# Expert gathering and scattering dealt out between weight pieces, and decode values and states in another matmul form, in a two-layer decoder step

## The reference, cut to what matters

```python
# per layer; x is prompt or sample
x = x + mixers(rmsnorm(x))        # 6 mLSTM + 6 SSD (pairs of 12 heads) + 4 retention units
x = x + cross_attn(rmsnorm(x))
x = x + ffn(rmsnorm(x))           # layer 0: dense SwiGLU; layer 1: top 2 of 8 experts
# a decode step of a mixer unit, for each of the 8 samples (all three kinds have this form)
S = decay * S + outer(v, k)       # a 128 x 128 state per sample and unit
y = S @ q
# experts
for e in range(8):
    act = silu(h @ w_gate[e]) * (h @ w_up[e])
    out = out + combine[..., e:e+1] * (act @ w_down[e])
```

## Time and profile before

| | us |
|---|---|
| median of 3 runs | 1915.89 (1913.73 to 1925.07) |
| the profiled execution | 1909.86, its span 1908.0 |
| PE busy over the span | 1808.2 (95%) |
| DVE, ACT, POOL busy | 1290.4, 1060.4, 367.7 |
| mixers' units, layer 0 and layer 1 | about 203 to 316 and 905 to 1019 |
| experts with their gatherings and scatterings | about 1236 to 1900 |

### The profile page before, as it was taken

One profiled execution on the slowest core, in us unless ns is written; L12 is line 12 of the kernel. 1 busy time (PEld: TensorE's weight loads), 2 busy tenths in 40 slices (PEclk: granted clock), 3 DMA queues, 4 the chain that ended last, 5 costly groups with the idle time before them and its releaser, 6 DMA issues.

```text
span 1908.0 us, 30795 instructions
## 1 busy us (share of the span) xinstructions
PE 1808.2 (95%) x12287; PEld 1648.4 (86%) x12287; DVE 1290.4 (68%) x1836; ACT 1060.4 (56%) x1709; POOL 367.7 (19%) x334
## 2 busy tenths in 40 slices
PE   7999989999899998999999999799899999989997
PEld 6999979997799998999989987688788888878886
DVE  4764776542556567655855533698879978978986
ACT  4445445443545454445445534377667866766775
POOL 4970332000000007932231000040012003000000
PEclk9999989999899998999979999899999999999999
DMA  7554345547655453553446367379959978986994
GB/s 296 177 172 163 122 141 182 200 170 288 226 175 193 168 207 126 191 180 134 144 124 248 134 248 292 121 267 355 358 212 350 370 259 298 363 330 228 355 363 167
DMA packets 73603, 434.07 MB, mean 227 GB/s; under 512 B 8373, under 2 KB 13045, under 8 KB 33013
## 3 DMA queue, kind: packets, MB, share of 16 engines
q1 hardware_dynamic: 71332, 425.19, 61.8%
q0 software_dynamic: 2128, 6.92, 1.0%
HBM read 407.59 MB, written 24.48 MB: 226 GB/s over the span
## 4 chain that ended last, share of the span: by engine, by line
PE 81%; DVE 10%; DMA 5%; ACT 2%; issue 1%; SPq 0%; DVEq 0%; ACTq 0%
PE ps L1134 16%; PE ps L576 14%; PE ps L577 14%; PE ps L578 13%; PE ps L1160 8%; DVE wL L301 3%; DMA ring<-x_down_dram 2%; PE ps L1117 2%; PE ps L556 2%; DVE stream L1886 2%; PE ps L816 1%; DMA ring<-x_gu_dram 1%; PE ps L1172 1%; DVE proj L1943 1%; PE ps L797 1%; ACT wH L295 1%
## 5 line engine op out<-in xcount | busy, mean ns | idle before, releaser
L301 DVE TENSOR_TENSOR wL<-ring,wH 128x1024 fp32r<-128x1024 f32 (+1 forms) x704 | 834.4, 1216 | 383.6 <-ACT wH L295 379.2
L295 ACT ACTIVATE wH<-ring 128x1024 fp32r<-128x1024 f32 (+1 forms) x704 | 709.1, 1026 | 280.2 <-PE ps L578 117.6
L576 PE MATMUL ps<-hH,wH 128*128 128x264 f32 x1376 | 400.7, 291 | 14.3 <-DVE hL L1669 7.8
L577 PE MATMUL ps<-hL,wH 128*128 128x264 f32 x1376 | 392.5, 285 | 0.0
L578 PE MATMUL ps<-hH,wL 128*128 128x264 f32 x1376 | 392.0, 285 | 0.0
L1134 PE MATMUL ps<-wH,projR 128*128 128x512 f32 (+1 forms) x1152 | 294.0, 377 | 0.3 <-ACT wH L295 0.3
L576 PEld LDWEIGHTS ps<-hH,wH 128*128 128x128 f32 x1376 | 261.1, 190 | 23.0 <-issue 19.0
L577 PEld LDWEIGHTS ps<-hL,wH 128*128 128x128 f32 x1376 | 261.7, 190 | 0.6
L578 PEld LDWEIGHTS ps<-hH,wL 128*128 128x128 f32 x1376 | 260.5, 189 | 0.0
L576 PE MATMUL ps<-projR,wH 128*128 128x264 f32 (+1 forms) x816 | 239.0, 293 | 15.8 <-DVE projR L2041 7.1
L1134 PEld LDWEIGHTS ps<-wH,projR 128*128 128x128 f32 x1152 | 211.0, 188 | 35.9 <-issue 1.4
(11 more groups left out here) (365 smaller groups left out, 2394.6 us busy)
## 6 DMA issues: line engine op xcount, KB each, us to landing
ring<-x_gu_dram SPq DMA_DIRECT2D x96, 1024.0 KB, 7.1
ring<-x_down_dram SPq DMA_DIRECT2D x60, 1024.0 KB, 7.0
ring<-w_in_dram SPq DMA_DIRECT2D x56, 1024.0 KB, 4.9
ring<-x_gu_dram SPq DMA_DIRECT2D x48, 768.0 KB, 5.7
ring<-w_gu_dram SPq DMA_DIRECT2D x22, 1024.0 KB, 4.9
stream<-states_dram SPq DMA_DIRECT2D x32, 512.0 KB, 4.2
ring<-w_out_dram SPq DMA_DIRECT2D x16, 1024.0 KB, 4.9
o_states_dram<-stream SPq DMA_DIRECT2D x32, 512.0 KB, 4.4
```

The source lines that it names most:

```text
L295: act.activation(wH[:, buf * PIECE:buf * PIECE + n], slot(s, half * n, n), ACT.Copy).then_inc(hi_ready, 1)
L301: dve.tensor_tensor(wL[:, buf * PIECE:buf * PIECE + n], slot(s, half * n, n), f32(wH[:, buf * PIECE:buf * PIECE + n]), ALU.subtract).then_ ...
L576: pe.matmul(dst, wh, high(k0 + k), start=k0 + k == 0, stop=False)
L577: pe.matmul(dst, wh, low(k0 + k), start=False, stop=False)
```

## The change

Two things are changed in one step.

**Experts.** `gather` and `scatter` take one k (of 8) at a time. PE's list puts gather k of the next group behind down piece k of the group's third item, `slot_sums` behind down piece 8, and scatter k of the last group behind gate and up piece k of the second chunk of the next group's first item. A gathering alternates between bank 7 and one gate bank instead of four banks. The last group's scattering becomes two jobs: items 9 and 10 behind the down pieces of item 11, and item 11 alone (8 times 2 matmuls) at the end. `turn_chunk` of a chunk moves from behind the eighth piece of the next chunk to behind its fourth. ACT's and DVE's parts of all this are dealt out likewise.

**Decode.** `spread` is two matmuls of 512 columns: a 0/1 column for the unit as stationary operand, and as moving operand a block diagonal matrix of the values of all units of a kind (`value_blocks`, one DVE instruction of 128 x 1024 for each kind and layer). `read_out` has q as stationary operand, repeated to 32 columns, and the state as moving one: 8 matmuls of 128 columns, each into 32 partitions, four beside each other. ACT copies the result (`copy_rows`, 128 x 256), PE transposes it in two (`turn_rows`), and DVE's `read_in` follows. The result of units 0 to 11 goes to bank 0, which `spread` uses as well; so `read_out(u)` waits for the first half of `update(u+1)`, and `spread(u)` for `read_in(u-2)`. In `ssd_d` the wait for `read_in` gives way to waits for `turn_rows` (and so for `copy_rows`) and for DVE's `outputs` of the unit before.

```diff
 def ml_d(h):
                     blocks3(bank(6, SEQ, SEQ), lambda st: ones, mS(h))
                     if h:
-                        pe.wait_ge(dec_y, l * UNITS + h)
+                        turn_rows(h - 1)
+                        pe.wait_ge(ml_state, n)
 def ssd_d(j):
+                    turn_rows(i - 1)
                     if j:
-                        pe.wait_ge(dec_y, l * UNITS + i)
+                        pe.wait_ge(ssd_h, n)
 def spread(u):
                         if u:
                             pe.wait_ge(dec_S, n - 1)
-                        for b in range(NB // 2):
-                            part, at = divmod((u - first) * NB + hf * (NB // 2) + b, 32)
-                            ins = pe.matmul(bank(hf, b * P, P), row_of(part, at), vrow[g][:, :], start=True, stop=True)
-                        ins.then_inc(dec_bc, 1)
+                        if hf == 0 and 0 <= u - 2 < NH + SP:
+                            pe.wait_ge(dec_y, l * UNITS + u - 1)
+                        one = constR[:, R_UNIT + u - first:R_UNIT + u - first + 1].to_broadcast([P, P])
+                        pe.matmul(bank(hf), one, values_of(l, g)[:, hf * 512:(hf + 1) * 512], start=True, stop=True).then_inc(dec_bc, 1)
 def read_out(u):
-                    pe.wait_ge(dec_S, 2 * (n + 1))
...
+                    if u < NH + SP:
+                        pe.wait_ge(dec_S, 2 * (n + 1) + 1)
...
-                    for b in range(NB):
-                        ins = pe.matmul(bank(read_bank(u), 448 + b, 1), state(u)[:, b * P:(b + 1) * P], q[:, b:b + 1], start=True, stop=True)
+                    for c_ in range(2):
+                        for r_ in range(4):
+                            b = 4 * c_ + r_
+                            ins = pe.matmul(read_rows(u, c_, r_), q[:, b:b + 1].to_broadcast([P, 32]), state(u)[:, b * P:(b + 1) * P], start=True, stop=True)
+                def turn_rows(u):
+                    pe.wait_ge(dec_row, l * UNITS + u + 1)
+                    for c_ in range(2):
+                        ins = pe.transpose(bank(read_bank(u), c_ * P, P), rows_in[:, c_ * P:(c_ + 1) * P], ident)
 PE, items
-                gather(0)
+                for k in range(KT):
+                    gather(0, k)
                 slot_sums(0)
                 for i in range(ITEMS):
+                    g = i // GROUP
                     for c_ in range(CHUNKS):
                         for k in range(KT):
                             gate_up(i, c_, k)
-                        if c_ == 0 and i and i % GROUP == 0:
-                            scatter(i // GROUP - 1)
-                        if c_:
-                            turn_chunk(CHUNKS * i + c_ - 1)
-                    if i % GROUP == GROUP - 1 and i < ITEMS - 1:
-                        gather(i // GROUP + 1)
-                        slot_sums(i // GROUP + 1)
+                            if c_ == 1 and i and i % GROUP == 0:
+                                scatter(g - 1, k)
+                            if c_ and k == 3:
+                                turn_chunk(CHUNKS * i + c_ - 1)
                     for f in range(F_TILES):
...
                         down(i, f)
-                scatter(GROUPS - 1)
+                        if i == ITEMS - 1 and f < KT:
+                            scatter(len(JOBS) - 2, f)
+                        elif i % GROUP == GROUP - 1 and f < KT:
+                            gather(g + 1, f)
+                        elif i % GROUP == GROUP - 1 and i < ITEMS - 1 and f == KT:
+                            slot_sums(g + 1)
 ACT, units
                     if i + 1 < UNITS:
                         weights_of(i + 1)
+                    if i:
+                        copy_rows(i - 1)
```

More of the change, by code:

```diff
@@ L76 @@
 N_ITEM_PIECES = ITEMS * ITEM_PIECES
+JOBS = [tuple(range(GROUP * g, GROUP * g + GROUP)) for g in range(GROUPS - 1)] + [(ITEMS - 3, ITEMS - 2), (ITEMS - 1,)]
 N_INFO = 1 + NE
@@ L350, in read_bank, with read_rows @@
         def read_bank(u):
[L352 removed]
+            return 0 if u < NH + SP else 6
+        rows_in = tmp[:, 1664:1920]
+        def read_rows(u, c_, r_):
+            return bank(read_bank(u), c_ * P, P, 32, 32 * r_)
         caP, caPT = conv[:, 0:512], conv[:, 1024:1536]
@@ L1107, in slot_sums, with gather @@
                     ins.then_inc(slots_mm, 1)
[L1109 to L1118 removed]
+                def gather(g, k):
+                    if k == 0:
+                        pe.wait_ge(place, g + 1)
+                        pe.wait_ge(rt_dve, TOK_LOW[2])
+                    b = gather_bank(g, k)
+                    take_bank(b, gx_lo, g * KT + k + 1)
+                    for n_, tt in enumerate((0, 0, 1, 1, 2)):
+                        ins = pe.matmul(bank(b, 0, SPAN), token_part(n_)[:, k * P:(k + 1) * P], place_part(tt), start=n_ == 0, stop=n_ == 4)
+                    ins.then_inc(gx, 1)
                 def gate_up(i, c_, k):
@@ L1408, in weights_of, with copy_rows @@
                         ret_e(i - NH - SP)
+                def copy_rows(u):
+                    n = l * UNITS + u
+                    act.wait_ge(dec_mv, 2 * n + 1)
+                    if u:
+                        act.wait_ge(dec_y, n)
+                    act.activation(rows_in, bank(read_bank(u), 0, 2 * P), ACT.Copy).then_inc(dec_row, 1)
                 weights_of(0)
@@ L1589, in _, with gather_high @@
                 QM = Q0 + piece_of["ffn"]
-                def gather_high(g):
-                    for k in range(KT):
-                        act.wait_ge(gx, g * KT + k + 1)
-                        act.activation(xg(0, k), bank(gather_bank(g, k), 0, SPAN), ACT.Copy).then_inc(gx_hi, 1)
+                def gather_high(g, k):
+                    act.wait_ge(gx, g * KT + k + 1)
+                    act.activation(xg(0, k), bank(gather_bank(g, k), 0, SPAN), ACT.Copy).then_inc(gx_hi, 1)
                 def silu(i, c_):
```

187 lines of the change are left out of this document (103 added, 84 removed).

## The result

The changed kernel takes 1898.5 us (median of five runs, 1897.43 to 1905.29); its ratio to the kernel before is 0.9925, with a 95% interval of 0.9897 to 0.9952. A second series gave 0.9915 (0.9884 to 0.9946). So by the ratios it is 14 to 16 us faster, where 29 us under the median was forecast; by the medians it is 16 to 20 (beside the two series the kernel before had 1918.89 and 1914.11). By the ratios it lies within the 1% that the prediction called the same. The profiled execution has a span of 1899.2 us against 1908.0.

A forecast was written before the change was run, and what follows sets the result against it. PE was taken to bound nearly everything. Experts -27 us and decode 0 turned 1909.86 into 1883 us for an execution like the profiled one, 1887 us as measured median; range 1862 to 1906.

The forecast's parts named there:

- Gatherings: Experts, tails of each group's third item: waits for bank 6 go, each tail 23.6 us, together -21.7 us.
- Scatterings: Experts, items with a scattering: dealt out, each leaves 5.84 us of work, -1.74 each, three of them -5.2 us.
- The last scattering: Experts, item 11 and the end: 32 of 48 matmuls move into item 11, the end shortens as much at most; 0.
- Decode, mLSTM: mLSTM units: read-out newly waits for the state update's first half through bank 0; +0.9 us a unit, +9 us.
- rival C: Decode, mLSTM and SSD: the clock falls behind the new wait, +12 to +23 us, 1899 to 1910; chance 0.17.
- Half clock before unit 6: Sign that the forecast is wrong: granted clock at 0.5 in mLSTM, before unit 6.
- Decode, SSD: SSD units: wait for `read_in` gives way to one for ACT's copy; -0.4 us a unit, -4 us (-9 to 0).
- Decode, retention and the end: Retention units: PE saves 1.26 us a unit, half counted for eight units; -5 us (-10 to 0).
- E: Rival, experts: DMA takes half of the experts' gain, 1900 us; chance 0.10.
- idle PE: Sign that the forecast is wrong: PE idle in the middle of a plain expert item.
- B: Rival, decode: shorter PE work counts everywhere, mLSTM stays at 6.53 us, SSD and retention gain -9 and -10; 1868 us, chance 0.14.
- D: Rival, experts: the dealt gathering itself stalls on its reused bank, 58 us, making 1945 us; chance 0.05.

The follow-up runs named there:

- fill_less: The changed kernel with four idle matmuls of 256 columns where PE waits in mLSTM and SSD; ratio to the kernel before 0.9919.
- after_again: The changed kernel itself, unaltered, measured a second time beside the kernel before; ratio 0.9915.
- decode_only: The kernel before with the decode half of the change alone, experts as before; ratio 1.0036.
- end_whole: The changed kernel with the last group scattered whole after item 11, as before; ratio to the kernel before 0.9898.
- values_new: The changed kernel with the old read-out of the states, keeping the block diagonal values and two-matmul spread; ratio to the kernel before 0.9807.

## Why the prediction was right and wrong, step by step

- **Gatherings, -21.7: right.** The tails take 24.4, 23.7 and 24.2 us (23.6 forecast) at a clock of 1.00, and 0.8 us is left of PE's 15.6 us of waits. Together -20.3.
- **Scatterings, -5.2: right.** Items of 53.64, 53.62 and 53.32 against 53.2, together -4.3.
- **The last scattering, 0: wrong by 1 to 2 us.** The working assumed that the end gets shorter by as much as item 11 grows. It does by 3.25; but item 11's down part grew by 5.18, since the dealt matmuls (3.9 us) also met a wait of 1.1 us for L2256, on a DVE that does its splits first.
- **Decode, mLSTM, +9: right in size, in part by luck.** Measured +9 to +10 for both layers, by other terms. The chain at full clock:

```profile
229.36 2.15 DVE L1944 SCALAR_TENSOR_TENSOR stream<-ps,kgate,stream 128x128 f32<-128x128 f32 x8
...
230.53 0.64 PE L840 MATMUL ps<-stream,proj 128*32 128x128 f32 x16 [2.05 <-DVE stream L1944]
...
231.11 0.49 PE L622 MATMUL ps<-nrm 128*128 128x128 f32 x2
...
233.41 0.42 DVE L2003 SCALAR_TENSOR_TENSOR proj<-ps,proj 128x256 f32<-128x256 f32 x1 [0.28 <-PE ps L720]
...
236.46 0.86 DVE L1944 SCALAR_TENSOR_TENSOR stream<-ps,kgate,stream 128x128 f32<-128x128 f32 x3
```

  From L1944 to L2003 4.05 us (4.38 forecast), a period of 7.10: +0.56 a unit and not +0.9, since `read_out` takes 0.58 (230.53 to 231.11) and not 1.0. At full clock that is +4.8 for both layers (42.65 a layer in `fill_less`, 40.25 before); the remaining 4 to 5.5 us are units that ran partly at half clock, 8.2 to 8.8 us long, one or two a layer. So the chain was priced too high, and rival C made up for it: it came as well, in three or four of the ten units, and its price of up to 2.5 us a unit was 1.1 to 1.7. Half clock before unit 6 was named as a sign of being wrong, and it is there (a mean of 0.92 in layer 0).
- **Decode, SSD, -4: near in size, not for its reason.** Measured -2 to -5 us for both layers, in the four profiles that have the whole decode change and ACT's old order (the changed kernel, `after_again`, `decode_only`, `end_whole`). The forecast saw that the copy stands behind L1346 (now L1385) and worked out 5.3 us for the way to the products; in the third unit it is 272.49 - 266.99 = 5.50. But the first five periods (from one unit's state update to the next one's) became no shorter: 80.7 us in both layers before, 81.0 to 83.4 in the four. The gain is in the last one, from unit 11 to unit 12: 16.1 us before, 11.2 to 11.8. And the forecast took the way through ACT as given: with the copy ahead of the weights SSD takes 10 us less a layer.
- **Decode, retention and the end, -5: wrong, +3 to +4.** This is the step that failed. It took PE as the bound, since PE was busy all of 25.30 us, gave half of PE's saving as the gain, and let ACT's longer list only limit that gain, not add a wait. PE did become shorter, but the copy put a wait on ACT's list into each unit, 1.89, 0.62, 0.62 and 0.92 us in layer 1; the first two:

```profile
1010.85 0.44 PE L847 MATMUL ps<-const,tmp 128*128 128x128 f32 x2 [1.89 <-ACT tmp L1455]
...
1017.09 0.44 PE L847 MATMUL ps<-const,tmp 128*128 128x128 f32 x2 [0.62 <-ACT tmp L1455]
```

```profile
1016.14 0.61 ACT L1401 ACTIVATE nrm<-ps,const 128x128 f32<-128x128 f32 x2
1016.64 0.39 ACT L1455 ACTIVATE tmp<-ps 128x256 f32<-128x256 f32 x1
```

  The best period is 5.84 us, where 6.22 stood before and 5.5 was forecast; the stage's first period takes 6.79 and 6.25 us where it took 5.14 and 5.13, the clock falls in layer 0, and the last unit's copy and transposes add 0.6 us a layer behind the stage. Since the step from SSD into retention became shorter and the next one longer, the two stages are best taken together: forecast -9 us for both layers with the end, measured -2.6 to +0.3 in the same four profiles and about 1.2 more behind the stage. With the copy ahead, periods are 5.05 to 5.8: the forecast 5.5 was the time of a kernel in which ACT doesn't hold the rows back.
- **The sum.** -27 and 0 became -25 and +7 by the runs of the halves, so 9 us of the forecast are missing, 11 to 13 by the ratios of the changed kernel itself. Of the rivals, C came in part. E did not come as a loss of half the gain; the experts' half alone gave nearly all of it, though their time scatters by 5 us from profile to profile and item 10, a plain one, has the idle PE that the prediction named as a sign of being wrong: it takes 47.4 to 49.6 us from profile to profile. B and D did not come: `values_new` shows that the shorter spread counts in SSD and retention, but the states' part took it back.

On the two changes of form at `read_out` the weight loads show (idle time in brackets):

```profile
1014.95 0.38 PEld L840 LDWEIGHTS ps<-stream,proj 128*32 128x32 f32 x16 [0.17 <-issue]
1015.53 0.30 PEld L622 LDWEIGHTS ps<-nrm 128*128 128x128 f32 x2 [0.20 <-issue]
```

0.17 and 0.20 us here, where the earlier trace rows had 0.33 and 0.41; over the changed kernel's read-outs the first lies between 0.12 and 0.35 where PE doesn't wait for an engine, the second mostly at 0.20. The Trainium skill (TensorEngine Tiling (Array Packing), Tiling Modes) says that a change of mode drains the engine; this trace agrees that the loading of weights pauses at both changes, and doesn't tell a drain from another reason.

## What to carry to other kernels

When a step is taken off the busiest engine and put through another one (here matmul rows, copied by ACT, turned by PE), what counts is where the new instruction stands in that engine's list: find what is ahead of it there, and whether the first engine can go on meanwhile. One line of ACT's order was worth 23 us here, and the wait that names it (PE for ACT's copy, 24.7 us in 18 pieces; 8.1 in 6 with the copy ahead) is in the list of waits. A stage in which an engine is busy all the time gives back a saving only up to the next engine's list; price that list with the new instruction in it before half of the saving is booked.

## What the runs showed of the hardware

A read-out of eight matmuls (16 instructions) of 128 columns, each into 32 partitions, takes 0.58 us at full clock from its first start to that of the next product (230.53 to 231.11), a third of the one-column form's 1.71 (223.67 to 225.38). At the pace of the six products of the earlier trace rows, 1.3 us for their twelve instructions, sixteen would take 1.7 us, so several of the small ones run beside each other. Idle matmuls that keep PE busy raise the granted clock (SSD 0.79 to 0.95), but part of them lay on the path, and they moved the whole time by less than this measurement tells; shortening the wait raised it to 0.99 and gave 23 us.
